# Thirteen single-pass products of the tokens' high parts, put ahead of the eleventh early block on TensorE

## The reference, cut to what matters

```python
q = (h @ peer_wq)                                   # 8 heads
v1, i1 = top_k(q1 @ sub_keys1.T, 16)                # per token and head
v2, i2 = top_k(q2 @ sub_keys2.T, 16)
top_s, pos = top_k(v1[:, None] + v2[None, :], 16)   # 16 experts of 128 * 128
gate = softmax(top_s)
a = gelu(einsum('td,tkd->tk', h, peer_u[eid]))      # up
out = einsum('tk,tkd->td', gate * a, peer_v[eid])   # down
```

## Time and profile before

| what | us |
|---|---|
| median of 3 runs (958.72 to 959.98) | 959.85 |
| the profiled execution | 962.24 |
| span of its instructions | 960.4 |
| outside the span | 1.84 |
| PE busy | 950.1 |
| DVE, ACT, POOL busy | 759.0, 480.7, 209.6 |

### The profile page before, as it was taken

How to read it: one execution, slowest core, us unless ns; L and a number is a source line. 1 busy time by engine, 2 the same in 40 slices (tenths; PEclk the granted TensorE clock), 3 DMA queues, 4 the chain that set the end, 5 groups by cost and what they waited for, 6 DMA issues and landing times.

```text
span 960.4 us, 16383 instructions
## 1 busy us (share of the span) xinstructions
PE 950.1 (99%) x5324; PEld 830.2 (86%) x5324; DVE 759.0 (79%) x1458; ACT 480.7 (50%) x851; POOL 209.6 (22%) x249
## 2 busy tenths in 40 slices
PE   9999999999999999999999999999999999999998
PEld 9998899997999988888888888888888888888887
DVE  6899759898999988887776777777777777777766
ACT  6576554423899963334434434444444444444342
POOL 3075138887777720000000000000000000000000
PEclk9999999999999999999999999999999999999999
DMA  9444138825444367775555555555555555555554
GB/s 293 150 132 132 46 111 288 214 63 180 150 135 132 119 224 242 242 243 201 175 192 201 175 197 196 178 197 192 179 201 187 179 206 182 186 206 176 188 203 155
DMA packets 73017, 174.20 MB, mean 181 GB/s; under 512 B 6144, under 2 KB 38528, under 8 KB 72720
## 3 DMA queue, kind: packets, MB, share of 16 engines
q1 hardware_dynamic: 72544, 171.50, 53.2%
q0 software_dynamic: 288, 2.10, 1.1%
q10 hardware_dynamic: 144, 0.08, 0.0%
HBM read 165.00 MB, written 6.55 MB: 179 GB/s over the span
## 4 chain that ended last, share of the span: by engine, by line
PE 74%; DVE 2%; DMA 1%; ACT 1%; issue 0%; SPq 0%; ACTq 0%; DVEq 0%
PE psum L1976 35%; PE psum L1956 17%; PE psum L1841 10%; PE psum L1959 9%; PE psum L1919 3%; DMA raw<-in_peer_v_dram 0%; DMA raw<-in_peer_u_dram 0%; DVE rr L1259 0%; PE psum L1541 0%; DVE big L1341 0%; DVE big L1131 0%; ACT rr L793 0%; ACT rr L685 0%; DVE big L1127 0%; DVE big L1166 0%
## 5 line engine op out<-in xcount | busy, mean ns | idle before, releaser
L1976 PE MATMUL psum<-rr 128*128 128x512 f32 x1536 | 366.5, 391 | 0.0
L1976 PEld LDWEIGHTS psum<-rr 128*128 128x128 f32 x1536 | 287.5, 188 | 59.7
L1956 PE MATMUL psum<-h_all,rr 128*128 128x512 f32 x744 | 266.5, 392 | 0.2 <-DVE rr L1171 0.2
L793 ACT ACTIVATE rr<-raw 128x1024 fp32r<-128x1024 f32 x97 | 102.8, 1060 | 242.5 <-PE psum L1976 238.8
L1259 DVE TENSOR_TENSOR rr<-raw,rr 128x1024 fp32r<-128x1024 f32 x97 | 118.8, 1225 | 125.8 <-ACT rr L793 125.7
L1959 PE MATMUL psum<-h_all,rr 128*128 128x256 f32 x744 | 192.9, 280 | 0.0
L1956 PEld LDWEIGHTS psum<-h_all,rr 128*128 128x128 f32 x744 | 139.7, 188 | 28.3 <-DVE rr L1171 0.8
L1959 PEld LDWEIGHTS psum<-h_all,rr 128*128 128x128 f32 x744 | 139.7, 188 | 7.3
L1841 PE MATMUL psum<-t32s,raw 128*128 128x256 f32 x544 | 126.6, 383 | 2.5 <-ACT gel L691 2.0
L685 ACT ACTIVATE rr<-raw 128x1024 fp32r<-128x1024 f32 x93 | 98.7, 1061 | 52.0 <-DMA raw<-in_peer_u_dram 49.2
L1171 DVE TENSOR_TENSOR rr<-raw,rr 128x1024 fp32r<-128x1024 f32 x92 | 112.2, 1219 | 3.6 <-ACT rr L685 3.5
(11 more groups left out here) (216 smaller groups left out, 1129.4 us busy)
## 6 DMA issues: line engine op xcount, KB each, us to landing
raw<-in_peer_v_dram SPq DMA_DIRECT2D x128, 512.0 KB, 3.6
raw<-in_peer_u_dram SPq DMA_DIRECT2D x127, 512.0 KB, 4.0
big<-in_w_in_dram SPq DMA_DIRECT2D x10, 1024.0 KB, 5.6
big<-in_peer_wq_dram SPq DMA_DIRECT2D x8, 1024.0 KB, 6.5
up_kept<-gel SPq DMA_DIRECT2D x34, 128.0 KB, 1.7
big<-in_w_out_dram SPq DMA_DIRECT2D x4, 1024.0 KB, 5.2
gel<-up_kept SPq DMA_DIRECT2D x32, 128.0 KB, 3.6
rr<-big POOLq DMA_DIRECT2D x2, 1024.0 KB, 11.3
```

Source lines behind the costliest of these rows:

```text
L793: act.activation(v_sp[s][:, 0, :], v_raw[s], ACT.Copy).then_inc(v_hi, 1)
L1956: return pe.matmul(both, ut[s][:, 0, k, :], ht[:, :, k, :], start=(k == 0), stop=(k == DK - 1))
L1976: i = pe.matmul(psum[:, 4 + 2 * t + n, :], g_sp[:, s, x, t * P:(t + 1) * P], v_sp[s][:, y, n * 512:(n + 1) * 512], start=(first and m == 0 ...
```

## The change

In the loop over blocks 6 to 11, thirteen products are issued when `e == EARLY_TOP - 4`, that is ahead of block 10's own waits and products. Nothing reads what they leave in bank 6. They wait for nothing and signal nothing. No other engine's code changes.

```diff
+            def stay_awake_rows():
+                row = psum[:, 6, :]
+                line = h_all[:, 0].rearrange("p k t -> p (k t)")
+                side, flat = line[:, 0:P], line[:, 0:512]
+                even = flat.rearrange("p (n a) -> p a n", a=2)
+                wide = flat.rearrange("p (n a) -> p a n", a=16)
+                same = line[:, 0:1].to_broadcast([P, 512])
+                twice = line[:, 0:SEQ].unsqueeze(2).to_broadcast([P, SEQ, 2])
+                short = flat.bitcast(BF16)
+                pe.matmul(row, side, flat, start=True, stop=True)
+                pe.matmul(row, side, flat, start=True, stop=True)
+                pe.matmul(row, side, same, start=True, stop=True)
+                pe.matmul(row.rearrange("p (a n) -> p a n", a=2), side, even, start=True, stop=True)
+                pe.matmul(row.rearrange("p (a n) -> p a n", a=16), side, wide, start=True, stop=True)
+                pe.matmul(row, side, line[:, 1:513], start=True, stop=True)
+                pe.matmul(row.rearrange("p (n a) -> p n a", a=2), side, twice, start=True, stop=True)
+                pe.matmul(psum[0:32, 6, :], line[:, 0:32], flat, start=True, stop=True)
+                pe.matmul(row, line[0:32, 0:P], flat[0:32], start=True, stop=True)
+                pe.matmul(row, short[:, 0:P], short[:, 0:512], start=True, stop=True)
+                pe.matmul(row, short[:, 0:P], short[:, 512:1024], start=True, stop=True)
+                pe.matmul(row, side, flat, start=True, stop=True)
+                pe.matmul(row, side, flat, start=True, stop=True)
             for e in range(PH - 2, EARLY_TOP - 2):
+                if e == EARLY_TOP - 4:
+                    stay_awake_rows()
                 early_up(e)
```

## The result

| | median us | executions |
|---|---|---|
| before | 959.78 (958.72 to 960.15) | 6 |
| with the thirteen products | 964.28 (962.74 to 965.0) | 6 |

The ratio is 1.0043, 95% interval 1.0029 to 1.0057: by the medians 4.5 us more, by the interval 2.8 to 5.5. The forecast was 962.8, 3.0 us more; the median lies 0.1 us above the upper end of the range (964.2). The sign and the mechanism were right; the cost was too low. The profiled execution took 964.99 us with a span of 963.2 (before: 962.24 and 960.4).

The account below looks back on a forecast made before the run. PE, busy 950.1 of 960.4 us, was taken as the bound, with no idle time ahead of block 10. Thirteen products at 0.229 us make 2.97, all arriving: 959.85 + 2.97 = 962.8 us, range 961.9 to 964.2.

Parts of the forecast that it names:

- The place: TensorE's 2.02 us wait for a Gelu is ahead of block 8; no idle time ahead of block 10, where products go.
- rival B: Ordinary executions wait at block 10 after all, so products fill 2.02 us and keep the clock up: 959.0 us; chance 0.04.
- The plain price: Each 512-column fp32r product ahead of block 10 costs 0.229 us, like the down products; thirteen cost 2.97 us.
- The stepping reads: Among the thirteen, `even` and `wide` skip elements; taken at 0.229 us each, with up to 0.64 more each kept for the range.
- Rival A: Some reads among the thirteen are dear: `wide` alone gives 963.5 us, `even` too 964.1; chance 0.20.
- the upper row: Upper price for a repeating or skipping read, from 512 float32 columns: 0.86 us, 0.64 more each.
- The narrow and bfloat16 ones: Products with 32 stationary columns, 32 rows or bfloat16, taken at 0.229 us; cheap ends of these give 962.4.
- The sum: Thirteen products at 0.229 us, 2.97 us, added to the unprofiled median 959.85: 962.8 us, 0.31% more.
- Passage to the end: Transposes, held by PE alone, move by 2.97 us; VectorE's last gate value moves 1.5, 2 us ahead; 2.97 of 2.97 arrives.
- The low clock: The stretch at 0.50 granted clock behind block 8's wait, 220.66 to 224.07, costing 1.8 us, stays after the change.
- Rival C: Low clock falls after 228 us in ordinary executions and the products prevent it, returning 1.8 us: 961.0; chance 0.07.
- The range: For the whole kernel, 961.9 to 964.2 us for 8 in 10, taking in two dear reads.

Follow-up runs that it names:

- the repeat: The changed kernel run again unchanged, beside the kernel before on one chip: 963.89 us, interval of the difference 3.8 to 6.6 us.
- ladder: Kernel with six products each of twelve kinds ahead of block 10 in place of the thirteen, for spacing alone; one execution, 981.1 us.

## Why the prediction was right, and where it was not

- *The place.* Right: the wait is ahead of block 8, counted from instructions and Gelus. The same products cost 1.5 us at block 8 and 4.1 at block 10 by medians on one chip (2.0 and 3.7 by traces), and rival B falls.
- *The plain price.* Right: 13 x 0.229 = 2.97 forecast, 2.96 measured, 5.94 for twenty-six.
- *The stepping reads.* The term that was most too small. I took 0.229 for `even` and `wide`, "the nearest row", and measured was 0.46 and 0.43. Rival A had the sign and the upper row bounded it (0.64 more each, 0.2 measured), but the rule of the Trainium skill (SBUF — State Buffer, the note on "cachelines") beside it picked `wide` alone. That the rival's sums (963.5 and 964.1) lie nearer to the measured 964.3 than the forecast is luck in part: its price per read was three times too high.
- *The narrow and bfloat16 ones.* I bounded them only from below their price. Their own rate is the plain one or near it (0.24, 0.27 with the entry, 0.22), but the two changes of form cost 0.27 us in the group. I had put them at nothing, from the gate stage alone, where only float32 and fp32r products of the same 128 rows alternate.
- *The sum.* 2.97 + 0.43 + 0.27, 3.68 before rounding, would have given 963.5. The median was 964.3, and 0.8 us remain. The interval holds 3.68, the four executions of the repeat at full clock gave 3.4, and the thirteen plain ones 2.8. The two traces of the changed kernel differ by 2.2 us ahead of the copy L696, so scatter of that size is there; that it made these 0.8 us of the median isn't shown.
- *Passage to the end.* Right in kind: transposes 3.81 us later than in the second trace of before, held by TensorE alone, and the span 3.1 longer. The reserve was larger than forecast: VectorE's last gate value was 2.4 us ahead of TensorE and not 2. It came 1.6 us later than in that trace, counted from the copy L696, where I had 1.5.
- *The low clock.* I treated it as part of every execution's profile, and wrote that the prediction is wrong if it goes. It is absent from the trace after, but not by the change: five of 80 executions of the kernel before have such a mean clock, its own second trace has no such stretch, and the products come after the place. Rival C has nothing to stand on, as there is hardly anything to give back. The sum itself did not rest on it, as it adds the cost to the median of unprofiled executions.
- *The range.* Too narrow above. Two executions of six in the repeat had the low clock and lay 3 us over the others, and with the scatter of single executions at full clock no room was left for small terms that all add.

## What to carry to other kernels

Before filling a wait, count which instance of the loop waits: ahead of block 8 eight products of 0.23 us are free, ahead of block 10 thirteen cost all they take. A wait named in one profile need not be worth its length: removing the 1 to 2 us here only moved TensorE's wait to VectorE's last gate value. An fp32r product of 512 columns whose streamed operand skips elements costs twice a contiguous one, even at the smallest step.

## What the runs showed of the hardware

- Streamed fp32r operand, 512 columns: 0.23 us contiguous, 0.22 with one element for all or each element twice, 0.43 to 0.46 with steps of 8 to 64 bytes.
- Going from products of 128 rows to 32 costs 0.2 us, and from 32 rows of fp32r to 128 of bfloat16 0.1 us (ladder); the weight load starts late there (0.45 and 0.37 us of idle time of the loader). Going from bfloat16 to fp32r at 128 rows, or from 128 stationary columns to 32, costs nothing.
- A stall of TensorE of 2.0 us was followed by 3.41 us at 0.50 in one trace of the kernel before; a stall of 2.3 us at the same place in the changed kernel, and one of 1.2 us in the second trace of the kernel before, were not.
